# Latent attention with its position-free queries and keys multiplied channel by channel

## The reference

```python
q_b = einsum('bsr,re->bse', rms_norm(c_q, mla_q_norm_g), w_uq)      # 512 -> 8 * (128 + 64)
q_nope, q_rope = q_b[..., :128], apply_rope(q_b[..., 128:], cos, sin)
kv = einsum('bsr,re->bse', rms_norm(c_kv, mla_kv_norm_g), w_ukv)    # 512 -> 8 * (128 + 128)
k_nope, v_b = kv[..., :128], kv[..., 128:]
k_rope = apply_rope(k_r, cos, sin)                                  # one for all heads
s = (q_nope . k_nope + q_rope . k_rope) * (128 + 64) ** -0.5        # causal, softmax over keys
o_b = softmax(s) . v_b * silu(z_b)
```

## Time and profile before

| | us |
|---|---|
| median of three runs | 1927.44 |
| profiled execution: its own time | 1927.67 |
| its span, first to last instruction | 1925.9 |
| PE busy (a share of 99%) | 1915.0 |
| DVE busy | 1432.9 |
| ACT busy | 1082.4 |

### The profile page before, as it was taken

One profiled execution on the slowest core, in us unless ns is written; L12 is line 12 of the kernel. 1 busy time (PEld: TensorE's weight loads), 2 busy tenths in 40 slices (PEclk: granted clock), 3 DMA queues, 4 the chain that ended last, 5 costly groups with the idle time before them and its releaser, 6 DMA issues.

```text
span 1925.9 us, 26620 instructions
## 1 busy us (share of the span) xinstructions
PE 1915.0 (99%) x9721; PEld 1624.3 (84%) x9721; DVE 1432.9 (74%) x2059; ACT 1082.4 (56%) x1598; POOL 46.3 (2%) x74
## 2 busy tenths in 40 slices
PE   9999999999999999999999999999999999999998
PEld 7888888888888888888888888888888888888886
DVE  7777675656777675656767766888878887889898
ACT  6555686655545676654644444555555555555554
POOL 1000030000000030000100000000000000000000
PEclk9999999999999999999999999999999999999999
DMA  9864455565665456455666455665666656666664
GB/s 345 309 209 131 147 154 155 152 204 188 209 208 165 141 162 177 142 164 186 210 186 195 154 165 185 185 186 178 203 185 188 192 185 187 191 222 193 203 195 164
DMA packets 248058, 361.29 MB, mean 188 GB/s; under 512 B 15504, under 2 KB 134496, under 8 KB 247456
## 3 DMA queue, kind: packets, MB, share of 16 engines
q1 hardware_dynamic: 246112, 353.15, 58.3%
q0 software_dynamic: 1568, 6.60, 1.0%
q10 hardware_dynamic: 288, 0.33, 0.0%
HBM read 356.88 MB, written 3.16 MB: 187 GB/s over the span
## 4 chain that ended last, share of the span: by engine, by line
PE 97%; DVE 1%; DMA 1%; ACT 0%; issue 0%; SPq 0%; DVEq 0%; ACTq 0%
PE acc L458 22%; PE acc L451 12%; PE acc L435 11%; PE acc L437 11%; PE acc L436 11%; PE acc L1204 4%; PE acc L1205 4%; PE acc L1203 4%; PE acc L1467 3%; PE acc L1465 3%; PE acc L1466 3%; PE aux L515 2%; PE aux L1134 1%; PE aux L1467 1%; PE aux L1465 1%; PE aux L1466 1%
## 5 line engine op out<-in xcount | busy, mean ns | idle before, releaser
L398 DVE TENSOR_TENSOR sb_w_lo<-sb_stage,sb_w_hi 128x1024 fp32r<-128x1024 f32 x476 | 583.1, 1227 | 273.1 <-ACT sb_w_hi L393 266.5
L393 ACT ACTIVATE sb_w_hi<-sb_stage 128x1024 fp32r<-128x1024 f32 x476 | 502.3, 1058 | 349.6 <-PE acc L451 123.0
L458 PE MATMUL acc<-sb_xT,sb_w_hi 128*128 128x512 f32 x1856 | 445.7, 391 | 0.0
L458 PEld LDWEIGHTS acc<-sb_xT,sb_w_hi 128*128 128x128 f32 x1856 | 340.8, 188 | 65.8
L451 PEld LDWEIGHTS acc<-sb_xT,sb_w_lo 128*128 128x128 f32 x1856 | 238.7, 191 | 9.3
L451 PE MATMUL acc<-sb_xT,sb_w_lo 128*128 128x256 f32 x1856 | 243.0, 283 | 0.0
L435 PE MATMUL acc<-sb_w_hi,sb_mT 128*128 128x512 f32 x544 | 217.3, 399 | 0.0
L437 PE MATMUL acc<-sb_w_hi,sb_mT 128*128 128x512 f32 x544 | 212.2, 390 | 0.0
L436 PE MATMUL acc<-sb_w_lo,sb_mT 128*128 128x512 f32 x544 | 212.1, 390 | 0.0
L435 PE MATMUL acc<-sb_w_hi,sb_xT 128*128 128x512 f32 x384 | 155.9, 406 | 0.0
L437 PE MATMUL acc<-sb_w_hi,sb_xT 128*128 128x512 f32 x384 | 150.0, 391 | 0.0
(11 more groups left out here) (437 smaller groups left out, 2872.6 us busy)
## 6 DMA issues: line engine op xcount, KB each, us to landing
sb_stage<-w_in SPq DMA_DIRECT2D x232, 512.0 KB, 4.1
sb_stage<-w_up SPq DMA_DIRECT2D x176, 512.0 KB, 3.9
sb_stage<-w_out SPq DMA_DIRECT2D x96, 512.0 KB, 4.0
sb_stage<-w_down SPq DMA_DIRECT2D x54, 512.0 KB, 6.8
sb_pair_stage<-w_down SPq DMA_DIRECT2D x34, 512.0 KB, 5.4
sb_kvb<-w_in SPq DMA_DIRECT2D x16, 512.0 KB, 6.2
sb_stage<-w_ukv SPq DMA_DIRECT2D x16, 512.0 KB, 3.8
sb_stage<-w_kv SPq DMA_DIRECT2D x15, 512.0 KB, 6.2
```

The costliest lines, as they stand in the source:

```text
L393: act.activation(w_hi[:, j % RING, 0:size], stage[:, j % RING, 0:size], ACT.Copy).then_inc(hi_ready, 1)
L398: dve.tensor_tensor(w_lo[:, j % RING, 0:size], stage[:, j % RING, 0:size], w_hi[:, j % RING, 0:size].bitcast(F32), ALU.subtract).then_inc( ...
L458: mm = pe.matmul(acc[:, 2 * pair + c, :], hi[:, k, c * P:(c + 1) * P], both, start=first and k == 0, stop=last and k == 3)
```

## The change

Queries and keys without position come out of the product with channels on the partitions (`product_latent_cols`), one unit of 256 columns (two heads) for each chunk: units 18 to 21 for the queries, 24 to 27 for the keys. The weights are rearranged outside the kernel so that these columns lie together. The positions of all queries are units 22 and 23, the values 28 to 31, both still by rows. The two halves of a column chunk are joined by an ACT copy of one half to `cols_half` (`copy_cols`) and a DVE addition of the other (`add_cols`), which frees the pair. Rows are copied by ACT without a scale (`copy_rows`). The norm of `c_kv` is applied to the latent before it is turned (ACT, step 18), that of `c_q` with the score scale in `mla_max` (`query_scale`). `rsqrt` moves from DVE's step 19 to its step 17, the turns of `c_kv` from units 18 and 19 to 19 and 21. The latent heads' turns (`MLA_TB`) and their copies to `qkT` are gone. A layer has 28 chunks in place of 24.

```diff
-DIFF_TB = [2, 3, 4, 7, 8, 11, 12, 13]
-C_TURN = {10: (0, 0, 5), 11: (0, 1, 6), 18: (1, 0, 9), 19: (1, 1, 10)}
+DIFF_TB = [2, 3, 4, 7, 8, 10, 12, 13]
+C_TURN = {10: (0, 0, 5), 11: (0, 1, 6), 19: (1, 0, 9), 21: (1, 1, 11)}
 QR_TB = 14
 KEY_HEAD = 4
-MLA_TB = [16, 17, 18, 21, 22, 25, 26, 29]
-GATE_TURN = {12: (0, 0, 19), 13: (0, 1, 20), 20: (1, 0, 23), 21: (1, 1, 24), 28: (2, 0, 27), 29: (2, 1, 28),
-             36: (3, 0, 30), 37: (3, 1, 31)}
-X_TB = 32
+GATE_TURN = {12: (0, 0, 16), 13: (0, 1, 17), 20: (1, 0, 18), 21: (1, 1, 19), 28: (2, 0, 20), 29: (2, 1, 21),
...
+QUERY_COLS, KEY_COLS = {18 + n: n for n in range(4)}, {24 + n: n for n in range(4)}
+C_QUERY, C_ROPE, C_KEY, C_VALUE, C_Z, C_OUT = 9, 13, 14, 18, 20, 24
...
+        def product_latent_cols(pe, base, j, k0, pair):
+
+
+            pe.wait_ge(lo_ready, base + (j + 1))
+            hi, lo = (w[:, j % RING, :].rearrange("p (k n) -> p k n", n=256) for w in (w_hi, w_lo))
+            tiles = [(k, c) for k in range(4) for c in range(2)]
+            for k, c in tiles:
+                pe.matmul(acc[:, 2 * pair + c, :], hi[:, k, c * P:(c + 1) * P],
+                          mT[:, k0 + k, :, :].rearrange("p h t -> p (h t)"), start=k == 0, stop=False)
+            for k, c in tiles:
+                mm = pe.matmul(acc[:, 2 * pair + c, 0:SEQ], lo[:, k, c * P:(c + 1) * P], mT[:, k0 + k, 0, :],
+                               start=False, stop=k == 3)
+            mm.then_inc(unit_used, 1)
...
+                        load(sp, base, U_QKV + 22 + i, rows(w_uq, 4, i, 2, WIDTH), 512)
+                    for n in range(4):
+                        load(sp, base, U_QKV + 24 + n, rows(w_ukv, 4, 0, 4, n * 256, 256), 256)
+                    for c in range(2):
                         for i in range(2):
-                            load(sp, base, U_QKV + 18 + 2 * c + i, rows(w_uq, 4, i, 2, c * 512), 512)
-                    for c in range(4):
-                        for i in range(2):
-                            load(sp, base, U_QKV + 24 + 2 * c + i, rows(w_ukv, 4, i, 2, c * 512), 512)
+                            load(sp, base, U_QKV + 28 + 2 * c + i, rows(w_ukv, 4, i, 2, WIDTH + c * 512), 512)
...
-                        pe.wait_ge(tb_free, tb0 + (MLA_TB[h] + 1))
+                        if h == 0:
+                            evacuated(pe, pairs, C_KEY + 2)
+                            evacuated(pe, pairs, C_KEY + 3)
+                            pe.wait_ge(tb_free, tb0 + QR_TB + 2)
+                            pe.wait_ge(pv_free, pv0 + 2 * HEADS)
                         pe.wait_ge(row_max, head0 + (HEADS + h))
                         for col, q, keys in ((0, 1, SEQ), (SEQ, 0, P)):
                             o = sc1[:, col:col + keys]
-                            pe.matmul(o, qkT[:, q * P:(q + 1) * P], qkT[:, 2 * P:2 * P + keys], start=True, stop=False)
+                            pe.matmul(o, query_of(h)[:, q * P:(q + 1) * P], key_of(h)[:, 0:keys], start=True, stop=False)
                             mm = pe.matmul(o, qrT[:, h // 2, q * P:(q + 1) * P], krz[:, h % 2, 0:keys],
                                            start=False, stop=True)
...
-                        if u >= 2 and r == 0:
-                            if 0 < h <= HEADS:
-                                mla_turn_weights(h - 1)
-                            if h < HEADS:
-                                turn(pe, tb0 + MLA_TB[h], mla_block(h))
+                        if u >= 2 and r == 0 and 0 < h <= HEADS:
+                            mla_turn_weights(h - 1)
...
-                        if u < 18:
-                            c, i, last_i = u // 8, u % 8, 7 if u < 16 else 1
-                        else:
-                            c, i, last_i = 3 + (u - 18) // 2, u % 2, 1
+                        c, i = u // 8, u % 8
+                        if u >= 18:
+                            c, i = C_ROPE - 6, u - 22
+                            if u in QUERY_COLS:
+                                c, i = C_QUERY - 6 + QUERY_COLS[u], 0
+                            if u in KEY_COLS:
+                                c, i = C_KEY - 6 + KEY_COLS[u], 0
+                            if u >= 28:
+                                c, i = C_VALUE - 6 + (u - 28) // 2, u % 2
                         if i == 0:
                             banks_free(pe, pairs, 6 + c)
...
+                        elif u in QUERY_COLS or u in KEY_COLS:
+                            product_latent_cols(pe, base, U_QKV + u, 0 if u < 24 else 4, c % 2)
                         else:
                             product_rows(pe, base, U_QKV + u, mT, (0 if u < 24 else 4) + 2 * i, 2, 512, c % 2,
-                                         i == 0, i == last_i)
+                                         i == 0, i == 1)
...
+                            if j == 1:
+                                pe.wait_ge(ckv_scaled, layer + 1)
...
-                        if u >= 2 and r == 0:
-                            if 0 < h <= HEADS:
-                                copy_weights(2 * HEADS + 2 * (h - 1))
-                            if h < HEADS:
-                                copy_bank(MLA_TB[h], qkT)
+                        if u >= 2 and r == 0 and 0 < h <= HEADS:
...
+                    def copy_cols(u, chunk):
+
+                        multiplied(act, quads * 4, U_QKV + u)
+                        if chunk not in (C_QUERY, C_KEY):
+                            evacuated(act, pairs, chunk - 1)
+                        pair = chunk % 2
+                        act.activation(cols_half[:, :, :], acc[:, 2 * pair:2 * pair + 2, SEQ:2 * SEQ], ACT.Copy)\
+                           .then_inc(cols_copied, 1)
+
+                    def copy_rows(u, chunk, dst):
+
+                        multiplied(act, quads * 4, U_QKV + u)
+                        for t in range(T):
+                            ins = act.activation(dst(t), acc[:, 2 * (chunk % 2) + t, :], ACT.Copy)
+                        ins.then_inc(acc_free[chunk % 2], 1)
+
...
                     for u in range(32):
+                        if u - 1 in QUERY_COLS:
+                            copy_cols(u - 1, C_QUERY + QUERY_COLS[u - 1])
+                        if u - 1 in KEY_COLS:
+                            copy_cols(u - 1, C_KEY + KEY_COLS[u - 1])
                         rounded(U_QKV + u)
+                        if u == 18:
+                            act.wait_ge(c_rstd, layer + 1)
+                            for t in range(T):
+                                ckv = qb[:, t, RANK:2 * RANK]
+                                ins = act.activation(ckv, ckv, ACT.Copy, scale=rstd_c[:, T + t:T + t + 1])
+                            ins.then_inc(ckv_scaled, 1)
...
-                        if u == 20 or (u > 20 and u % 2 == 1):
-                            c = (u - 19) // 2
-                            act.wait_ge(c_rstd, layer + 1)
-                            multiplied(act, quads * 4, U_QKV + 19 + 2 * c)
-                            for t in range(T):
-                                r = (0 if c < 3 else T) + t
-                                dst = qb[:, t, c * 512:(c + 1) * 512] if c < 3 else \
-                                    kvb[:, t, (c - 3) * 512:(c - 2) * 512]
-                                ins = act.activation(dst, acc[:, 2 * ((9 + c) % 2) + t, :], ACT.Copy,
-                                                     scale=rstd_c[:, r:r + 1])
-                            ins.then_inc(acc_free[(9 + c) % 2], 1)
+                        if u == 24:
+                            copy_rows(23, C_ROPE, rope_rows)
+                        if u == 30:
+                            copy_rows(29, C_VALUE, value_rows(0))
                     for u in range(32):
+                        if u == 0:
+                            copy_rows(31, C_VALUE + 1, value_rows(1))
...
+                        dve.scalar_tensor_tensor(out=s[:, 0:SEQ], in0=sc1[:, 0:SEQ], scalar=query_scale[:, 1:2],
+                                                 in1=causal[:, :], op0=ALU.mult, op1=ALU.add)
+                        step(dve.scalar_tensor_tensor(out=s[:, SEQ:SEQ + P], in0=sc1[:, SEQ:SEQ + P],
+                                                      scalar=query_scale[:, 0:1], in1=causal[:, P:2 * P],
+                                                      op0=ALU.mult, op1=ALU.add))
...
+                    def add_cols(chunk, dst):
+
+                        dve.wait_ge(cols_copied, layer * 8 + (chunk - C_QUERY if chunk < C_ROPE else chunk - C_KEY + 4) + 1)
+                        pair = chunk % 2
+                        dve.tensor_tensor(dst, acc[:, 2 * pair:2 * pair + 2, 0:SEQ], cols_half[:, :, :], ALU.add)\
+                           .then_inc(acc_free[pair], 1)
+
                     add_rows_qkv(5)
                     dve.wait_ge(bias_back, 16)
                     for u in range(32):
+                        if u - 1 in QUERY_COLS:
```

(14 more changed lines are left out.)

82 lines of the change are left out of this document (44 added, 38 removed).

## The result

The changed kernel takes 1938.33 us (median of five, 1937.82 to 1938.47), the kernel before in the same job 1927.97: 10.4 us more, a ratio of 1.0051 with the interval 1.0039 to 1.0062. It is slower, as forecast; the forecast was 1933.5, with 1931.4 to 1936 as its own range and 1929.5 to 1940 as the whole one. The time lies in the whole range only. The profiled execution has a span of 1936.6 us, 10.7 more than before.

A forecast was written before the change was run, and what follows sets the result against it. PE was taken to bound the kernel: waits of 12.0 us in two layers plus 1.0 for column units less 7.0 for turns gave +6.0, 1933.5 us. Own range 1931.4 to 1936, whole range 1929.5 to 1940.

The forecast's parts named there:

- What bounds it: PE is busy throughout the stage, so each PE instruction removed is gained in full and each wait lost in full.
- POOL's stretch: Rival: DVE runs slower beside POOL over units 25 to 28, up to 1.8 us a layer, giving 1937; chance 0.13.
- three signs of being wrong: No PE idle time at units 19 and 25, waits under 5 us a layer, or a drop of the granted clock.
- The gain: PE saves the latent heads' 16 turns at 0.44 us each, 7.0 us in all; lower bound 5.8.
- The column units: Column units cost PE 0.06 us more than row units; 16 of them make +1.0 us in both layers.
- Unit 19: PE waits for DVE's rope key read-out, delayed behind rsqrt and diff_max: 3.3 us a layer with the pause, lower bound 1.2.
- Unit 25: PE waits for ACT's copy of the rope rows, queued behind the copy of head 6's turn: 2.1 us a layer.
- The small ones: Short PE waits a layer: 0.2 us at unit 24, 0.3 at unit 27, 0.1 at the first gate unit.
- The clock: Rival: the granted clock falls to half in PE's wait at unit 19 in each layer, +7 us, 1940.5; chance 0.06.
- Only one hole: Rival: the wait at unit 19 or that at unit 25 does not come out, +1.2 us, 1928.6; chance 0.12.
- read-outs in time: Rival: copies and additions end before PE asks; with small waits alone -4.8 us, 1922.6; chance 0.07.
- the range's lower end: 1929.5: a wait of 1.2 us at unit 19 and 2.1 at unit 25, nothing else, for +2 us.

The follow-up runs named there:

- b1_no_turns: The kernel before without the latent heads' turns by PE and ACT's copies of their bank (scores read stale operands); 1921.79 us, ratio 0.9965.
- e5_all_open: `e4_both` with the copies and additions of units 19, 25 and 26 moved into their own steps; 1923.96 us, ratio 0.9979 to the kernel before.
- e4_both: Changed kernel with rsqrt, key read-out and unit 18's copy and addition moved earlier, and rope rows copied first in ACT's step 24; 1929.21 us, ratio 1.0005.
- f2_pool_later: `e4_both` with POOL starting to turn the queries' positions only when unit 25 has been added; 1927.24 us, ratio 0.9996 to the kernel before.
- b2_rsqrt_at_17: The kernel before with only rsqrt moved from DVE's step 19 to step 17, ahead of diff_max; 1932.32 us, ratio 1.0021.
- e1_key_first: Changed kernel with DVE reading the rope key out at the end of step 17, ahead of rsqrt and diff_max; 1937.68 us, ratio 1.0048.

## Why the prediction was right, and where it was short

*What bounds it.* Right. PE is busy without a gap in both open stages, and 6.4 us of its work taken out (`b1_no_turns`) were 6.4 us gained. The lost time appeared in full as well.

*The direction.* Right, and its cause too: PE waits at the two places that were named, released by the instructions that were named. The size was not: 6.0 us forecast, 10.4 measured, beyond the forecast's own range. The time is inside the whole range because that reached up for two other cases, POOL's stretch and most of the clock's. And one of the three signs of being wrong came, the granted clock dropped.

*The gain.* 7.0 forecast, 6.4 measured. I took the chain's 0.44 for a turn; the spacing that I named beside it, 0.36, and the pause behind it come to 0.40.

*The column units.* +1.0 forecast, 1.7 measured to the end of the stage, 2.2 by the medians of `e5_all_open` and `b1_no_turns`, which also hold the 0.2 a layer ahead of unit 18.

*Unit 19.* Right in place, cause and size (3.3 forecast, 3.2 measured): DVE's instructions follow each other from 687.32 to 692.42 as the old durations had it. *Unit 25.* Right in place and cause, 0.2 too long: two copies took 1.08 us, not the 1.27 of the earlier trace rows, which scale as they copy. *The small ones.* 0.4 in place of 0.6, all of it at unit 27.

*The clock* is the step that failed. I wrote that a wait of 3.3 us is shorter than the silence at the program's end, behind which the clock had fallen, that the dense work on either side speaks against a fall, and gave it 0.06. But the rows there said only that it was full at 1916 and half at 1922; they bound the silence that suffices from above and say nothing of 3 us. The windows between, in the same trace of the kernel before, would have misled even more:

```profile
1920.00:1921.00 1.00, 0.00 (x0) 0.00 (x0) 0.86 (x4) 0.26 (x1) 0.00 (x0) 1.00 0.81 332
1921.00:1922.00 1.00, 0.00 (x0) 0.00 (x0) 0.82 (x2) 1.00 (x2) 0.00 (x0) 0.95 0.00 0
```

PE's last matmul had ended at 1916.9, and the clock was full for 5 us more; in the stage of the change a silence of 3.05 us was enough. The fall came, in both layers, and cost 1.6 us each, 3.2 of the 4.4 us by which I was short. My bound of 3.5 us a layer was twice what it took; it set the bar of two matmuls (1.19) against the spacing of two (0.45), where a bar of two at full clock is 0.62 (0.23 + 0.39). By the Trainium skill (TensorE: Matmul & The Clock Gate, section HAM oscillation) waits inside a kernel can put the clock back to half and the following work starts cold; here the trace agrees, unit 19 took 4.47 us from start to start where 2.9 is usual, and my 0.06 rested on no row with a wait of this length.

*POOL's stretch.* Rightly left out for the changed kernel: beside POOL the same small instruction of `diff_max` took 0.31 there instead of 0.17, and the wait at unit 27 is 0.3. It would have cost 0.8 a layer had the rope rows been copied in time, as `e4_both` and `f2_pool_later` show.

*The other rivals.* Only one hole, and read-outs in time: both fell, the waits come from the written order, and only a new order took them away. The price of the first was also added up wrongly: without unit 25's wait 3.9 us a layer remain, without unit 19's 2.7, on average 3.3 and not 3.6, so +0.6 and not +1.2. So was the range's lower end: 1.2 and 2.1 alone make 2 x (3.3 + 0.5 - 3.5) = +0.6, and its +2 needs turns worth 5.8 besides.

## What to carry to other kernels

When a product's chunk shrinks from two units to one, its banks are asked for one unit sooner: walk the order of every engine that reads them out, place by place, with the durations of the old trace. In the changed kernel that gave each wait within 0.2 us. It must be done anew for each new order: the 1.2 us before unit 21 and the 1.75 us of `b2_rsqrt_at_17` I missed. Opening the largest wait shows the next in its shadow, so count them all before pricing the repair: 9.5 promised, 7.0 got, and the whole gain only when the two waits behind it were opened as well. And where PE will stand still for about 3 us or more in a dense stretch, charge a fall of the clock behind it (1.6 us here) until a trace shows otherwise.

## What the runs showed of the hardware

The clock fell behind waits of 3.05 us and, in `e1_key_first`, 2.92 us, in both layers each time, and not behind waits of 1.96, 1.66, 1.20 and 0.80 us in the same dense stage. What lies between 1.96 and 2.92 no run shows. It fell only after PE had started again (full in 245.00:246.00, 0.56 in 246.00:247.00), stayed low for some 3.4 us and cost 1.6. Useless matmuls in the wait avoided it and made the program 3.1 us shorter. A four-column instruction on DVE took 0.99 us instead of 0.17 beside POOL, and 0.31 in another kernel, each time until POOL's instruction ended. Waits of up to 1.0 us at the program's last units differ from one trace to another without following an edit.
